# Input norms from token-major squares, a transposed output stage and a pad ahead of the activation buffers

## What is computed

```python
def rmsnorm(x, g):
    xf = x.astype(jnp.float32)
    y = xf * lax.rsqrt(jnp.mean(xf * xf, axis=-1, keepdims=True) + NORM_EPS)
    return (y * g.astype(jnp.float32)).astype(x.dtype)

def memory_attention(q, mem, mem_g, w_mem_kv):
    mn = rmsnorm(mem, mem_g)
    kv = (mn @ w_mem_kv).reshape(b, m, 2, MEM_HEADS, HEAD_DIM)
    ...

def pool_layer(x, mem, norm_g, w_in, ...):
    h = rmsnorm(x, norm_g)
    proj = h @ w_in
    ...
def second_block(x, ...):
    ...
        x = x + jnp.einsum('bsf,fd->bsd', jax.nn.silu(g) * u, w_down[l])
    return rmsnorm_2(x, final_norm)
```

## Time and profile before

| | |
|---|---|
| time, median of 3 runs | 2088.69 us (2088.55 to 2091.04) |
| the profiled execution | 2088.68 us, of it the span 2086.9 us |
| TensorE busy | 2051.0 us, 98% |
| VectorE, ScalarE, GpSimd busy | 1482.5, 1021.6, 483.1 us |
| DMA | 370 MB, 177 GB/s in the mean |

### The profile page before, as it was taken

The page is one execution under the profiler, slowest core; times in us unless marked ns, Lnnn a source line. Parts: engine busy times, 40 slices in busy tenths (PEclk is TensorE's granted clock), DMA queues, the critical chain, the costliest instruction groups (busy, mean ns, idle before and its releaser), DMA issues.

```text
span 2086.9 us, 29262 instructions
## 1 busy us (share of the span) xinstructions
PE 2051.0 (98%) x11470; PEld 1754.1 (84%) x11470; DVE 1482.5 (71%) x2056; ACT 1021.6 (49%) x1508; POOL 483.1 (23%) x442
## 2 busy tenths in 40 slices
PE   7999999999999999999999999999999999999997
PEld 6788888888788888888878888888888888888886
DVE  8866778789777556876656668777776557777765
ACT  5445444466533554654455555444444344454443
POOL 8305553300000344330212225211010000110122
PEclk9999999999999999999999999999999999999998
DMA  7555566566654333555444445555556665555664
GB/s 251 171 185 156 178 188 197 184 207 221 221 179 160 119 104 122 183 198 191 162 153 150 144 149 186 188 182 188 185 187 181 186 193 184 189 183 184 184 186 131
DMA packets 104089, 370.03 MB, mean 177 GB/s; under 512 B 11632, under 2 KB 12944, under 8 KB 103824
## 3 DMA queue, kind: packets, MB, share of 16 engines
q1 hardware_dynamic: 103952, 368.16, 55.2%
HBM read 366.02 MB, written 2.10 MB: 176 GB/s over the span
## 4 chain that ended last, share of the span: by engine, by line
PE 92%; DVE 6%; ACT 1%; issue 0%; POOL 0%; DMA 0%; DVEq 0%; ACTq 0%
PE psg L531 51%; PE psg L533 24%; DVE s_w L1622 2%; PE psg L578 2%; PE psg L580 2%; PE psg L579 2%; PE psg L530 2%; PE pst L531 1%; PE pst L617 1%; DVE s_rh L1640 1%; PE pst L533 1%; DVE s_ry L1640 1%; PE pss L793 1%; PE pso L813 0%; ACT s_w L1084 0%
## 5 line engine op out<-in xcount | busy, mean ns | idle before, releaser
L1622 DVE TENSOR_TENSOR s_w<-s_stage,s_w 128x1024 fp32r<-128x1024 f32 (+2 forms) x699 | 871.1, 1247 | 368.8 <-ACT s_w L1084 365.6
L1084 ACT ACTIVATE s_w<-s_stage 128x1024 fp32r<-128x1024 f32 (+2 forms) x699 | 728.3, 1043 | 789.2 <-PE psg L531 423.7
L531 PE MATMUL psg<-s_ry,s_w 128*128 128x512 f32 x2656 | 939.0, 401 | 3.7 <-DVE s_mv L1689 2.5
L533 PE MATMUL psg<-s_ry,s_w 128*128 128x256 f32 x2486 | 698.7, 281 | 0.0
L531 PEld LDWEIGHTS psg<-s_ry,s_w 128*128 128x128 f32 x2656 | 490.9, 189 | 116.3 <-issue 4.1
L533 PEld LDWEIGHTS psg<-s_ry,s_w 128*128 128x128 f32 x2486 | 470.8, 189 | 7.3
L531 PE MATMUL psg<-s_rh,s_w 128*128 128x512 f32 x1280 | 458.6, 404 | 11.9 <-DVE s_rh L1640 9.5
L533 PE MATMUL psg<-s_rh,s_w 128*128 128x256 f32 x1180 | 332.4, 282 | 0.0
L531 PEld LDWEIGHTS psg<-s_rh,s_w 128*128 128x128 f32 x1280 | 237.9, 189 | 65.2 <-issue 8.1
L531 PE MATMUL psg<-s_hid,s_w 128*128 128x512 f32 x704 | 245.9, 399 | 0.0
L533 PEld LDWEIGHTS psg<-s_rh,s_w 128*128 128x128 f32 x1180 | 224.6, 190 | 3.7
(11 more groups left out here) (388 smaller groups left out, 2224.8 us busy)
## 6 DMA issues: line engine op xcount, KB each, us to landing
s_stage<-in_wo SPq DMA_DIRECT2D x96, 512.0 KB, 3.5
s_stage<-in_wg SPq DMA_DIRECT2D x88, 512.0 KB, 3.5
s_stage<-in_wu SPq DMA_DIRECT2D x88, 512.0 KB, 3.6
s_stage<-in_ain SPq DMA_DIRECT2D x64, 512.0 KB, 3.6
s_stage<-in_wd SPq DMA_DIRECT2D x64, 448.0 KB, 3.4
s_stage<-in_wkv SPq DMA_DIRECT2D x32, 512.0 KB, 4.0
s_stage<-in_wd SPq DMA_DIRECT2D x32, 512.0 KB, 3.5
s_stage<-in_bq SPq DMA_DIRECT2D x24, 512.0 KB, 3.5
```

The costliest lines, as they stand in the source:

```text
L531: m = e.matmul(o, M.WH[:, r, ws], xx, start=begin, stop=end)
L533: m = e.matmul(o[:, T:2 * T], M.WL[:, r, ws], xh, start=False, stop=False)
L1084: e.activation(M.weights(c, 0, n), M.staged(c, n), ACT.Copy).then_inc(S["wh"], 1)
L1622: e.tensor_tensor(M.weights(c, 1, n), M.staged(c, n), M.weights(c, 0, n), ALU.subtract).then_inc(S["wl"], 1)
```

## The change

**Pad.** `PAD` is allocated behind `LV`; its size brings the next tensor, `RY`, to 512 modulo 1024 bytes. Two small buffers `CSQ` and `CSM` come before it.

**Input norms.** `mem` and `x` are also loaded token-major (`memt`, `xt`, 2 MB each, tokens on the partitions) into `TM`. ScalarE squares them in place in pieces of 512 columns with an accumulated sum (8 activations each), VectorE adds the four partial sums, the rsqrt is taken on two columns. For `RB`, VectorE multiplies the identity by the column, and TensorE multiplies this diagonal matrix by ones (two matmuls of 128 columns). GpSimd's squares of `mem` and `x` go.

**Start.** Unit 0 is loaded by ScalarE's queue in two halves and split in halves (`first`); the memory comes in six pieces instead of five (`MEMP`), the vectors in two, the first with one gain only; the splits of units 1 and 2 stand behind the eight first tiles of `MEM` on ScalarE and VectorE. The DMA order changes.

**End.** TensorE transposes `X` (gain applied) into all eight PSUM banks, 32 transposes of 128x128, the first eight ahead of the last square. The sum for the norm is only taken as two columns. ScalarE and VectorE copy each four pieces of 128x512 from PSUM with the token's scale into `OT`; eight stores write the result token-major.

```diff
+MEMP = ((0, 1), (1, 2), (2, 4), (4, 8), (8, 12), (12, 16))
-NORM = {n: i for i, n in enumerate(("mem", "mem_c", "x", "kv", "kv_c", "eff", "eff_c", "eff_a", "ffn", "fin"))}
+NORM = {n: i for i, n in enumerate(("mem_c", "x_c", "kv", "kv_c", "eff", "eff_c", "eff_a", "ffn", "fin"))}
@@ Memory
+        self.CSQ = fix("csq", [128, 2, 2, 4])
+        self.CSM = fix("csm", [128, 2, 2])
...
+        self.PAD = fix("pad", [128, (512 - (nc.sbuf_base + 31) // 32 * 32) % 1024 // 4])
...
+        self.TM = alloc(l00, "tm", [128, 2, D])
...
+        self.OT = alloc(ff, "ot", [128, 2, D])
@@ tensor_program
+    def token_rows(n, ticks):
+        for _ in range(ticks):
+            yield
+        i = NORM[n]
+        vacant(("o", i % 2))
+        w.wait_ge("eps", 5)
+        w.wait_ge("nr_dg", i + 1)
+        for t in range(2):
+            m = e.matmul(M.PSO[i % 2][:, t * 128:t * 128 + 128], ones, M.NW[:, t * 128:t * 128 + 128], start=True, stop=True)
+        m.then_inc(S["nr_mm"], 1)
...
-    side.start(mem_norm())
+    side.start(token_rows("mem_c", 15))
     group([("mk", 0, j) for j in range(4)], H, ready("m0"))
     pair(("mv", 0), H, ready("m0"))
     side.start(lam())
+    side.start(token_rows("x_c", 13))
     group([("mk", 1, j) for j in range(4)], Y, ready("m1"))
     pair(("mv", 1), Y, ready("m1"))
-    w.wait_ge("sqx", KT)
-    norm_rows("x", [(ones, M.ACC[1][:, :])])
...
+    def turn(q, t):
+        for j in range(4 * q, 4 * q + 4):
+            w.wait_ge("xg", j + 1)
+            m = e.transpose(result(P, M, t, q)[:, 128 * (j % 4):128 * (j % 4) + 128], M.X[:, j, 128 * t:128 * t + 128], ident)
+        m.then_inc(S["turned"], 1)
...
     w.wait_ge("sql", 15)
+    sums(M.ACC[1], True)
+    turn(0, 0)
+    turn(0, 1)
     w.wait_ge("sq15", 1)
-    norm_rows("fin", [(ones, M.ACC[1][:, :]), (ones, M.YT[0][:, :])])
+    sums(M.YT[0], False).then_inc(S["nr_mm"], 1)
+    for q in (1, 2):
+        turn(q, 0)
+        turn(q, 1)
+    w.wait_ge(*P.out[("wd", 1), KT - 1])
+    turn(3, 0)
+    w.wait_ge("nr_dve", 3 * NORM["fin"] + 1)
+    turn(3, 1)
@@ scalar_program
+    def token_norm(n, rc, ticks):
+        i = NORM[n]
+        for _ in range(ticks):
+            yield
+        for t in range(2):
+            w.wait_ge(f"l_tm{i}", 16)
+            for q in range(4):
+                src = M.TM[:, t, 512 * q:512 * q + 512]
+                x = e.activation(src, src, ACT.Square, accum_out=M.CSQ[:, i, t, q:q + 1])
+            x.then_inc(S["sqt"], 1)
+            yield
...
+    for half, name in enumerate(("st_a", "st0")):
+        ws = slice(512 * half, 512 * half + 512)
+        e.dma_start(M.ST[:, 0, ws], P.units[0][0][:, ws]).then_inc(S[name], 16)
     tables()
+    w.wait_ge("l_vec0", 16)
+    for j in range(8):
+        w.wait_ge(mem_piece(j), 16)
+        high(M.RH, j, M.MEM[:, j, :], M.vec("mg0", j), "m0")
+        if j in (0, 2):
+            first(j // 2)
+    split()
     split()
...
+    side.start(token_norm("mem_c", 0, 9))
     nxt(8)
...
+    side.start(token_norm("x_c", 1, 7))
...
+    for q in range(4):
+        w.wait_ge("turned", 2 * q + 1)
+        e.activation(M.OT[:, 0, 512 * q:512 * q + 512], result(P, M, 0, q), ACT.Copy, scale=M.RC[1][:, 0:1]).then_inc(S["fin_act"], 1)
@@ vector_program
+    def token_norm(n, rc, ticks):
...
+        w.wait_ge("sqt", 2 * i + 2)
+        e.tensor_reduce(M.CSM[:, i, :], M.CSQ[:, i, :, :], AX.X, ALU.add).then_inc(S["csm"], 1)
...
+        for t in range(2):
+            x = e.tensor_scalar(M.NW[:, t * 128:t * 128 + 128], M.con("ident", 128), M.RC[rc][:, t:t + 1], None, ALU.mult)
+        x.then_inc(S["nr_dg"], 1)
@@ pool_program
-    for j in range(8):
-        w.wait_ge(("l_mem0", "l_mem1", "l_mem2", "l_mem2")[j // 2], 16)
-        square(M.ACC[0][:, :], j, M.MEM[:, j, :], "sqm")
-    side.start(mem_rest())
     ticks(16)
-    for j in range(KT):
-        w.wait_ge(f"l_x{j // 4}", 16)
-        square(M.ACC[1][:, :], j, M.X[:, j, :], "sqx")
@@ sync_program
+    e.dma_start(M.V[:, 0:16], A["vec"][:, 0:16]).then_inc(S["l_vec0"], 16)
+    for n in range(3):
+        memory(n)
     weights()
+    memory(3)
     weights()
+    e.dma_start(M.V[:, 16:NVEC], A["vec"][:, 16:NVEC]).then_inc(S["l_vec"], 16)
     weights()
+    memory(4)
+    memory(5)
+    weight_units(4)
+    e.dma_start(M.C[:, :], A["con"]).then_inc(S["l_con"], 16)
     weights()
+    e.dma_start(M.TM[:, :, :], A["memt"]).then_inc(S["l_tm0"], 16)
+    weight_units(2)
...
     for g in range(4):
         e.dma_start(M.X[:, 4 * g:4 * g + 4, :], A["x"][:, 4 * g:4 * g + 4, :]).then_inc(S[f"l_x{g}"], 16)
+        weight_units(2)
+    w.wait_ge("sqt", 2)
+    e.dma_start(M.TM[:, :, :], A["xt"]).then_inc(S["l_tm1"], 16)
```

More of the change, by code:

```diff
@@ L619, in transposes @@
         held["t", 0] = held["t", 1] = ("at_pt", n + 1)
-    def mem_norm():
-        for _ in range(9):
+    def token_rows(n, ticks):
+        for _ in range(ticks):
             yield
[L624 to L627, removed]
+        i = NORM[n]
[5 more added lines that the diff above has]
+        m.then_inc(S["nr_mm"], 1)
+        held["o", i % 2] = ("nr_rb", i + 1)
     def lam():
@@ L1064, in tensor_program, with sums @@
         residual(("wd", hv), both(M.HID), ready("hid", 22 * hv), (0, 1, 2), 2, (8, 7, 7))
+    side.drain()
+    def turn(q, t):
[3 more added lines that the diff above has]
+        m.then_inc(S["turned"], 1)
+    def sums(acc, begin):
+        for t in range(2):
+            m = e.matmul(M.PSO[NORM["fin"] % 2][:, t:t + 1], acc[:, 128 * t:128 * t + 128], ones[:, 0:1], start=begin and t == 0, stop=not begin and t == 1)
+        return m
+    last = P.bank[("wd", 1), KT - 1]
+    vacant(("s", 0), ("s", 1), ("t", 0), ("t", 1), ("o", 0), ("o", 1), ("g", 1 - last[1]))
     w.wait_ge("sql", 15)
+    sums(M.ACC[1], True)
+    turn(0, 0)
+    turn(0, 1)
     w.wait_ge("sq15", 1)
-    norm_rows("fin", [(ones, M.ACC[1][:, :]), (ones, M.YT[0][:, :])])
-    side.drain()
+    sums(M.YT[0], False).then_inc(S["nr_mm"], 1)
[6 more added lines that the diff above has]
+    turn(3, 1)
 def scalar_program(e, S, P, M):
@@ L1135, in silu, with first @@
         e.activation(M.ET[i % 2][:, :], M.ZT[i % 2][:, :], ACT.Tanh).then_inc(S["z_t"], 1)
+    def first(half):
+        done[0], ws = 1, slice(512 * half, 512 * half + 512)
+        w.wait_ge(("st_a", "st0")[half], 16)
+        e.activation(M.WH[:, 0, ws], M.ST[:, 0, ws], ACT.Copy).then_inc(S[("wh_a", "wh")[half]], 1)
     def mem_rest():
@@ L1729, in mem1, with first @@
             yield
+    def first(half):
+        done[0], ws = 1, slice(512 * half, 512 * half + 512)
+        w.wait_ge(("wh_a", "wh")[half], 1)
+        e.tensor_tensor(M.WL[:, 0, ws], M.ST[:, 0, ws], M.WH[:, 0, ws], ALU.subtract).then_inc(S[("wl_a", "wl")[half]], 1)
+    def token_norm(n, rc, ticks):
+        i = NORM[n]
+        for _ in range(ticks):
+            yield
+        w.wait_ge("sqt", 2 * i + 2)
+        e.tensor_reduce(M.CSM[:, i, :], M.CSQ[:, i, :, :], AX.X, ALU.add).then_inc(S["csm"], 1)
+        yield
+        yield
+        refine(n, M.RC[rc][:, :], M.CSM[:, i, :], M.CW[:, 0:2], EPV[0] * D)
+        normed(n)
+        w.wait_ge("l_con", 16)
+        if i:
+            w.wait_ge("nr_mm", i)
+        for t in range(2):
+            x = e.tensor_scalar(M.NW[:, t * 128:t * 128 + 128], M.con("ident", 128), M.RC[rc][:, t:t + 1], None, ALU.mult)
+        x.then_inc(S["nr_dg"], 1)
     def mem_norm():
[L1732 removed]
+        yield from token_norm("mem_c", 0, 11)
+        for _ in range(5):
             yield
[L1734 to L1738 removed]
+        w.wait_ge("nr_rb", 1)
         for j in range(4):
@@ L2132, in vector_program @@
     side.start(setup())
+    side.start(token_norm("x_c", 1, 9))
     nxt(4)
```

123 lines of the change are left out of this document (51 added, 72 removed).

## The result

The changed kernel takes 2069.55 us (median of 4 runs, 2069.31 to 2069.88), the one before 2088.62 us; the ratio is 0.9906, 95% interval 0.9889 to 0.9924. The profiled execution took 2069.31 us, its span is 2067.5 us. The forecast was 2071.8 us, its own range 2066 to 2078: the total lies 2.3 us from the forecast, but all three terms of the sum are off: the middle by 4.8 us one way, the start and the end by 2.3 the other.

A forecast was written before the change was run, and what follows sets the result against it. VectorE was taken to bound the start, while TensorE was busy nearly throughout the middle. From 2088.7 us, 12.6 for the start, 0 for the middle and 4.3 for the end came off: 2071.8 us, range 2066 to 2078.

The forecast's parts named there:

- Middle: First qm matmul to last product: the pad moves the activation buffers' addresses, taken to be worth 0.
- its own criterion: Middle: the prediction would be wrong if first qm to last product was not 1956.5 us within 2.
- The failed step: Middle: pair paces 0.347 and 0.353 occur at the same addresses, so a phase locks in; pad taken as 0.
- Rival (a): Middle: the pad works, pairs go to the fast level, 20.5 us less, 2051.3 us; chance 0.24.
- Rival (c): Middle: the new residue puts pairs on a slower level, about 29 us, 2101 us; chance 0.05.
- Start: Before the first qm matmul: 14.6 us won, 2.0 lost to ScalarE's squares, so 12.6 won; bounds 7 and 17.
- The mis-sized step: Start: mem tiles 4 to 7, behind 2.0 MB, there at 8.5 us, with 1.9 MB in by 8 us.
- The half clock beyond unit 1's start: Start: one half clock stretch kept after the sparse beginning, costing 1.7 us.
- The squares on ScalarE: Start: four activations take 3.4 us in one tick, twice, stalling 1 us each time: 2.0 us lost.
- The rest is 2.9 us: Start: 0.8 us left for lam, four ones-matmuls of 128 columns and small changes.
- Rival (b): Start: splits and token-major loads stall TensorE at both squares, two more half clock stretches, 2080.8 us; chance 0.09.
- End: After the last product: stores are last, 5.3 us at 394 GB/s, end at 2082.5; 4.3 us won, bounds 2.5 and 5.5.

The follow-up runs named there:

- the changed kernel at 896: The changed kernel with its pad resized so the activation buffers start at 896 modulo 1024, as in the kernel before; 2072.33 us.
- the two changed kernels at distance 0: The changed kernel with activation buffers at 896 modulo 1024, 2072.33 us; the changed kernel with weights moved to 256 and buffers kept at 512, 2071.36 us.
- the three at 128: The changed kernel itself, buffers at 512 modulo 1024, 2069.55 us; the changed kernel with buffers at 0, 2069.35 us, and at 768, 2070.07 us.
- 96: The changed kernel without the pad, buffers at 992 modulo 1024, distance to the weights 96 modulo 256; 2067.92 us.
- 64: The changed kernel with activation buffers at 64 modulo 1024, distance to the weights 192 modulo 256; 2076.99 us.

## Why the prediction was right, and where it was not

**Middle: wrong.** Predicted 0, found 4.8 us in the profile; by its own criterion (1956.5 us within 2) the step failed. Both traces have 3.4 us at half clock in this stretch, so the 4.8 are not the clock, and the kernel before with the pad alone has 4.7 at a like clock. In whole times the pad's address is worth less: 2.9 us on the kernel before (interval 1.7 to 5.2), 2.8 between the changed kernel at 896 and at 512. One part of that is the start: `qm` begins at 102.35 and 102.90 us in the two changed kernels at distance 0 and at 103.25 to 104.66 in the three at 128, where the 192 `pair` matmuls alone take 0.9 us more (worked out from the distances of the kernel before and the changed one). The rest was not separated. The failed step is the inference from the earlier trace rows: both levels occur at one address, so it is a phase and not an address. The 0.347 and 0.353 are two places in a pattern of unequal distances, and the distance to the weights sets which pattern runs: the commonest distances are 350, 361 and 349 ns at 0 modulo 256, 354, 346 and 353 at 128, 349 and 351 at 96. Two levels at one address say nothing of the mean at another. Rival (a), pairs at the fast level for 20.5 us, did not come: neither the change's address nor any other tried runs at that level throughout, the lowest mean is 350.12 ns. Rival (c), a slower residue, exists (64) but the change did not pick it. The Trainium skill (SBUF — State Buffer, on the two separate sides of SBUF) says that TensorE's ports never wait on anyone; 497.23 against 493.15 us in stretch F for the same matmuls differ by the placement of two operands of TensorE itself, which that sentence does not cover. Why the distance counts was not tried, nor were the distances 32, 160 and 224.

**Start: the mechanism right, 1.65 us too good.** That VectorE bound the start because it ran beside GpSimd's squares is shown by the run that keeps them. The terms: the first matmul came at 6.07, not 5.3 (0.8), as tile 0 was there at 4.90 instead of 4.2. Unit 1 began at 14.77, which after 6.07 and 2.8 us of work is 5.9 us lost instead of 4.4. The mis-sized step is the arrival of tiles 4 to 7, put at 8.5 and found at 10.8 us, although the rate was near the one assumed (1.75 MB by 8 us, where 1.9 were taken): in the changed kernel

```profile
0.00:10.80 10.80, 3.39 (x7) 1.92 (x8) 3.15 (x6) 4.14 (x7) 0.64 (x9) 1.00 0.76 269
```

had moved 10.8 x 0.269 = 2.9 MB when they came, 0.8 more than the 2.1 MB issued up to them. Loads issued later had taken their share, so a sum of the bytes ahead is only a lower bound. The half clock beyond unit 1's start cost 1.0 us (three pairs in 16.80 - 14.77 = 2.03 instead of 1.06), predicted 1.7. The squares on ScalarE cost nothing where 2.0 were taken: four start 0.61 us apart and take 2.5 us, not 3.4, and no wait of TensorE follows them; the lower bound given, "if the activations take 0.6 in all", was the case. The rest is 2.9 us instead of 0.8: 0.6 in the wait for the `mv` copies ahead of `qm` (the last row of the start's timeline), 1.0 in 192 `pair` matmuls at 232.4 ns, where the sum had 227, less 0.2 in the 128 pairs at 351.4 instead of 353; what makes up the other 1.5 I did not separate. Rival (b), stalls at both squares with more half clock, did not come.

**End: right, 0.7 too good.** From the end of the last product (2056.34) the scale took 3.16 us (predicted 3.0); the stores flowed from 2061.10, 4.76 behind it (4.5), for 5.57 us at 376 GB/s in the mean, where 5.3 at the 394 of the earlier trace rows were put, and 0.84 us pass from their last byte to the end where 0.6 were put. (The prediction's own times, 2086.9 and 2082.5, give 4.4 us and not 4.3.) That the stores are last and not the copies is right: the last copy ends at 2062.26, the span at 2067.5. The eight issues (4.04 us) end before the flow does.

**The sum.** 10.95 + 4.80 + 3.63 = 19.4 us instead of 16.9: the start and the end 2.3 short, the middle 4.8 over. That the errors run opposite ways is luck. The forecast's range, 12 us wide, held by its width: with 0 in the middle the same start and end would have given 2074.1, inside it too. It says little of whether the three steps were right.

## What to carry to other kernels

Look at where the stationary and the moving operand start relative to each other: here another distance modulo 256 bytes moved the kernel by up to 9 us (2067.92 to 2076.99, of it 1.7 clock), and a few sizes of pad tell the best in one profile each. Two paces of the same loop at one address do not rule out that the address matters; read the whole pattern, and compare means. Before two traces of one stretch are compared, compare their time at half clock: here 3.4 us more of it hid 1.7 of the pad's 4.7. Before a start is tuned, put the loads in the order in which they are needed and take the bytes ahead as a lower bound on the arrival, and look for work on GpSimd that slows VectorE's.
